# Hybrid decoder layer on one core: the gated delta rule's triangular inverse with 16x16 blocks solved on VectorE, all four token tiles together

## The reference

```python
lower = jnp.where(strict, jnp.einsum("bhnid,bhnjd->bhnij", kb, kc) * decay, 0.0)
a_mat = lower + jnp.eye(C, dtype=F32)
rhs = jnp.concatenate([vc * bc, kb * jnp.exp(gc)[..., None]], axis=-1)
sol = lax.linalg.triangular_solve(a_mat, rhs, left_side=True, lower=True, unit_diagonal=True)
```

## Time and profile before

| | us |
|---|---|
| median of 3 runs | 585.76 (583.97 to 585.95) |
| the profiled execution | 584.36 |
| its span | 582.5 |
| PE, PEld busy | 556.0, 422.6 |
| DVE, ACT, POOL busy | 263.5, 192.7, 183.2 |

### The profile page before, as it was taken

The page is one execution under the profiler, slowest core; times in us unless marked ns, Lnnn a source line. Parts: engine busy times, 40 slices in busy tenths (PEclk is TensorE's granted clock), DMA queues, the critical chain, the costliest instruction groups (busy, mean ns, idle before and its releaser), DMA issues.

```text
span 582.5 us, 11328 instructions
## 1 busy us (share of the span) xinstructions
PE 556.0 (95%) x4579; PEld 422.6 (73%) x4579; DVE 263.5 (45%) x632; ACT 192.7 (33%) x409; POOL 183.2 (31%) x126
## 2 busy tenths in 40 slices
PE   8999999999999999999999999999999999978894
PEld 6988887899999777577899996656565566544541
DVE  6598543683357334756411363322333232221126
ACT  6655545532223524446353221111111111111113
POOL 3353434164676436224534001121111112110020
PEclk9999999999999999999999999999999999999998
DMA  8865543513220320047988788999999999999975
GB/s 330 347 221 159 184 125 113 145 38 111 74 73 2 110 73 2 1 146 279 340 317 338 249 321 342 404 428 431 423 424 425 427 423 425 425 422 429 414 316 225
DMA packets 32083, 152.67 MB, mean 262 GB/s; under 512 B 8759, under 2 KB 12511, under 8 KB 25376
## 3 DMA queue, kind: packets, MB, share of 16 engines
q1 hardware_dynamic: 27360, 143.77, 63.7%
q0 software_dynamic: 4528, 8.15, 3.7%
q10 hardware_dynamic: 144, 0.03, 0.0%
HBM read 143.78 MB, written 16.27 MB: 275 GB/s over the span
## 4 chain that ended last, share of the span: by engine, by line
PE 67%; DMA 20%; DVE 4%; issue 4%; POOL 2%; ACT 2%; SPq 0%; DVEq 0%; POOLq 0%; ACTq 0%
PE bank L803 31%; DMA xg<-h2d,tok 11%; DMA w<-in_expert_w_dram 8%; PE bank L859 7%; PE bank L1249 6%; PE bank L1208 3%; PE bank L1223 2%; PE bank L828 2%; PE bank L1147 2%; PE bank L1161 1%; PE bank L1141 1%; PE bank L1261 1%; PE bank L1117 1%; POOL wlo L1578 1%; PE bank L966 1%
## 5 line engine op out<-in xcount | busy, mean ns | idle before, releaser
L1578 POOL TENSOR_TENSOR wlo<-raw,whi 128x1024 fp32r<-128x1024 f32 (+1 forms) x24 | 59.4, 2475 | 76.9 <-ACT whi L1278 72.2
L1705 POOL DMA_INDIRECT yd<-oy,dst x15 | 15.1, 1009 | 163.8 <-DVE oy L2249 153.1
L1208 PE MATMUL bank<-w,xT 128*64 128x256 f32 x512 | 58.2, 380 | 3.5 <-issue 3.5
L1223 PE MATMUL bank<-w,xT 128*64 128x256 f32 x512 | 58.2, 380 | 3.4 <-DMA w<-in_expert_w_dram 3.3
L1249 PE MATMUL bank<-w,hidT 128*64 128x512 f32 x256 | 58.5, 599 | 1.4 <-ACT hidT L1555 1.4
L1208 PEld LDWEIGHTS bank<-w,xT 128*64 128x64 f32 x512 | 37.3, 137 | 27.5 <-issue 12.0
L803 PE MATMUL bank<-wlo,hHi 128*128 128x256 f32 (+2 forms) x192 | 55.9, 291 | 0.0
L2227 DVE SCALAR_TENSOR_TENSOR hid<-bank,slot,sa 128x256 f32<-128x256 f32 x16 | 10.8, 674 | 94.5 <-issue 92.0
L1223 PEld LDWEIGHTS bank<-w,xT 128*64 128x64 f32 x512 | 36.5, 137 | 22.7 <-DMA w<-in_expert_w_dram 4.8
L803 PE MATMUL bank<-whi,hHi 128*128 128x256 f32 (+1 forms) x176 | 51.0, 290 | 0.2 <-POOL wlo L1578 0.2
L803 PE MATMUL bank<-whi,hLo 128*128 128x256 f32 (+1 forms) x176 | 49.6, 282 | 0.0
(11 more groups left out here) (388 smaller groups left out, 1132.2 us busy)
## 6 DMA issues: line engine op xcount, KB each, us to landing
w<-in_expert_w_dram SPq DMA_DIRECT2D x43, 2048.0 KB, 22.0
raw<-in_w_in_dram SPq DMA_DIRECT2D x24, 512.0 KB, 4.0
w<-in_expert_w_dram SPq DMA_DIRECT2D x10, 1024.0 KB, 7.3
yd<-zt SPq DMA_DIRECT2D x8, 512.0 KB, 5.0
yt<-yd SPq DMA_DIRECT2D x4, 1024.0 KB, 8.2
raw<-in_w_in_dram SPq DMA_DIRECT2D x6, 520.0 KB, 5.6
xt<-in_turned_dram SPq DMA_DIRECT2D x4, 512.0 KB, 6.8
X<-in_x_dram SPq DMA_DIRECT2D x4, 512.0 KB, 10.3
```

Source lines behind the costliest of these rows:

```text
L1208: m = pe.matmul(pb[3][r, 0:FF], xT[:, c, r], w1[u % 4][:, e, c * FF:(c + 1) * FF], start=(c == 0), stop=(c == KC - 1), skip_group_check=True)
L1223: m = pe.matmul(pb[7][r, 0:FF], xT[:, c, r], w3[u % 4][:, e, c * FF:(c + 1) * FF], start=(c == 0), stop=(c == KC - 1), skip_group_check=True)
L1578: pool.tensor_tensor(low_of(g), raw_of(g), high_of(g).bitcast(F32), ALU.subtract).then_inc(wlo_done, 1)
L1705: pool.indirect_dma_start(yd.ap()[:, :], bass.IndirectOffsetOnAxis(ap=dst_i[o][:, 0:1].bitcast(U32), axis=0), oy[o][:, :], None, bounds_ch ...
```

## The change

Levels 0, 1 and 2 of the inverse are no longer done by matmuls. The 16x16 diagonal blocks of all four tiles are inverted by back substitution on VectorE. `prep` masks Nm to its 16x16 blocks and sums them into `diag` (128 rows x 8 head-tiles x 16); SP writes `diag` to DRAM and reads it back in eight reads of 16 partitions each, so that each partition holds all 16 rows of its block (`spread`, one buffer for both pairs). `solve` then does 15 steps of one multiply and one sum, each waiting for the one before, and places the result in Xc. Levels 3 and 4 and the last one handle both pairs at once (8 blocks and not 4 per product, in Xc[i] with i the tile within its pair). The tasks of tiles 2 and 3 (`dec`, `decx`, `prep`) stand behind granule 18, the solves behind 19 and 21, level 3 starts behind 24, the last level behind 26, the `fin`s behind 27 and 28; nothing is left behind 29. In SP's stream the write of the blocks stands behind the load of granules 21 and 24, the reads behind 22 and 25; the second reads wait for the end of the first solve; the load of the key rows cB moves from behind 19 to behind 27. GpSimd's wait before granule 19's subtraction is for the block sums and not for the finished transposes. The core of the diff:

```diff
+SB = 16
+SOLVED = 3
...
 AFTER[17] += [("kt", 3), ("ktv", 3), ("prep", 0)]
+AFTER[17].append(("qg", 0))
+AFTER[18] += [("dec", 2), ("dec", 3), ("decx", 2), ("prep", 2)]
+AFTER[19] += [("qg", 2), ("solve", 0)]
+AFTER[21].append(("solve", 1))
 AMID = {g: {} for g in range(GR_IN)}
-for _i in range(LEVELS - 1):
-    AFTER[18 + _i].append(("lvY", 0, _i))
-    AMID[19 + _i][1] = [("lvX", 0, _i)]
-AFTER[23].append(("last", 0))
-AFTER[23] += [("dec", 2), ("dec", 3), ("decx", 2)]
-AFTER[24] += [("fin", 0), ("prep", 2)]
-for _i in range(LEVELS - 1):
-    AMID[25 + _i][2 if _i == 0 else 0] = [("lvY", 1, _i)]
-    AFTER[25 + _i].append(("lvX", 1, _i))
-AFTER[26].append(("silu",))
-AFTER[29] += [("last", 1), ("fin", 1)]
+AFTER[24].append(("lvY", 3))
+AMID[25][1] = [("lvX", 3)]
+AFTER[25].append(("lvY", 4))
+AMID[26][0] = [("lvX", 4)]
+AFTER[26] += [("lastY",), ("silu",)]
+AMID[27][0] = [("lastU",)]
+AFTER[27].append(("fin", 0))
+AFTER[28].append(("fin", 1))
+BLOCKS_OUT, BLOCKS_IN, KEYS_IN = {21: 0, 24: 1}, {22: 0, 25: 1}, 27
...
-    put("nM1", -((row % 2 == 0) & (blk == row + 1)).astype(np.float32))
+    put("blk16", -(row // SB == blk // SB).astype(np.float32))
+    put("unit16", -(row % SB == np.arange(SB)[None, :]).astype(np.float32))
     put("id64", row == blk)
     lv = []
-    for n in range(LEVELS - 1):
+    for n in range(SOLVED, LEVELS - 1):
...
+        Nm = [at(f"Nm{t}", [P, NH, P], (R4 if t < 2 else R8 + 4 * KB) + t % 2 * 2 * KB) for t in range(T)]
+        Xc, Uc, Yc = ([at(f"{n}{i}", [P, 2 * NH, HB], R4 + (o + 2 * i) * KB) for i in range(2)] for n, o in (("Xc", 4), ("Uc", 8), ("Yc", 12)))
+        Ym, Dm = ([at(f"{n}{i}", [P, NH, P], R4 + (o + 2 * i) * KB) for i in range(2)] for n, o in (("Ym", 12), ("Dm", 16)))
+        Um = [at(f"Um{i}", [P, 2 * NH, P], R4 + (16 - 8 * i) * KB) for i in range(2)]
+        spread = at("spread", [P, SB, 2 * NH, SB], R9)
...
+        eights = lambda a: sml(a, 2 * NH * SB).rearrange("p (c n) -> p c n", c=2 * NH)
+        diag, prods, inv = [eights(640), eights(768)], eights(896), eights(80)
...
+            def blocks_out(pr):
+                sp.wait_ge(rows_done, pr + 2)
+                sp.dma_start(nbd.ap()[pr], small[:, 640 + 128 * pr:768 + 128 * pr]).then_inc(s_bw, 16)
+
+            def blocks_in(pr):
+                sp.wait_ge(s_bw, 32 + 16 * (pr + 1))
+                if pr:
+                    sp.wait_ge(uinit, pr)
+                for d in range(P // SB):
+                    src = nbd.ap()[pr:pr + 1, d * SB:(d + 1) * SB, :].rearrange("o k n -> o (k n)")
+                    sp.dma_start(spread[d * SB:(d + 1) * SB, :, :, :].rearrange("p k c n -> p (k c n)"),
+                                 src.broadcast_to([SB, SB * 2 * NH * SB])).then_inc(s_spread, 16)
+
             sp.wait_ge(zero_set, 1)
             for g in range(5, GR_IN + 4):
                 granule(g)
+                if g in BLOCKS_OUT:
+                    blocks_out(BLOCKS_OUT[g])
+                if g in BLOCKS_IN:
+                    blocks_in(BLOCKS_IN[g])
                 if g == 11:
...
-                if g == 19:
+                if g == KEYS_IN:
+                    sp.wait_ge(uinit, 2)
                     keys_in()
...
-                for h in range(NH):
+                for c in range(2 * NH):
                     for i in range(2):
                         for r in (UP, DN):
-                            m = mm(banks[i][out(i, r), h * HB:(h + 1) * HB], stationary(i, h, r), moving(i, h, r))
-                            if h == NH - 1 and r is DN:
+                            m = mm(banks[i][out(i, r), c * HB:(c + 1) * HB], stationary(i, c, r), moving(i, c, r))
+                            if c == 2 * NH - 1 and r is DN:
                                 end(m, names[i])
...
+                    lv = k[1]
+                    if lv > SOLVED:
+                        for i in range(2):
+                            wait_read(pe, ("Xp", i, lv - 1))
+                    else:
+                        pe.wait_ge(uinit, 2)
+                    quarters([("Y", i, lv) for i in range(2)], lambda i, c, r: Nm[2 * (c // NH) + i][r, c % NH, r],
+                             lambda i, c, r: Xc[i][r, c, :], lambda i, r: OTHER[r.start] if i else r)
...
+                    pe.wait_ge(u_turned, lv - SOLVED + 1)
+                    quarters([("Xp", i, lv) for i in range(2)], lambda i, c, r: Uc[i][r, c, :],
+                             lambda i, c, r: Yc[i][r, c, :], lambda i, r: OTHER[r.start] if i else r)
...
+                elif k[0] == "lastU":
+                    lv = LEVELS - 1
                     for i in range(2):
-                        t = 2 * pr + i
-                        wait_read(pe, ("Y", t, lv))
-                        pe.wait_ge(um_low, t + 1)
-                        blocks(("Up", t, lv), lambda h, r, o: mm(o, Yc[i][DN, h, :], Um[i][DN, h, DN]), (UP,))
+                        name = ("Up", i, lv)
+                        wait_read(pe, ("Y", i, lv))
+                        pe.wait_ge(um_low, i + 1)
+                        ps = begin(name)
+                        for c in range(2 * NH):
+                            m = mm(ps[UP, c * HB:(c + 1) * HB], Yc[i][DN, c, :], Um[i][DN, c, DN])
+                        end(m, name)
                 elif k[0] == "fin":
...
-                    if k[1] == 0:
-                        decay_rows(0)
+                    decay_rows(k[1])
...
-                if k[0] == "prep":
+                if k[0] == "qg":
...
-                elif k == ("decx", 0):
-                    masked(0)
-                    masked(1)
+                elif k[0] == "decx":
+                    for t in (k[1], k[1] + 1):
+                        if k[1]:
+                            wait_read(pool, ("KK", t - 2))
+                        masked(t)
...
-                if ("fin", 0) in AFTER[g]:
-                    for t in (2, 3):
-                        wait_read(pool, ("Up", t - 2, LEVELS - 1))
-                        masked(t)
-                for t in (0, 2):
-                    if ("prep", t) in AFTER[g]:
-                        pool.wait_ge(uinit, t + 2)
+                if ("prep", 0) in AFTER[g]:
+                    pool.wait_ge(rows_done, 2)
...
+                    if t >= 2:
+                        wait_read(dve, ("QK", t - 2))
...
+                    pr = k[1] // 2
+                    blocks = Uc[pr]
                     for i, t in enumerate(tiles):
                         wait_read(dve, ("KK", t))
                         for r in (UP, DN):
-                            j = dve.tensor_tensor(Yc[i][OTHER[r.start] if i else r, :, :], Nm[i][r, :, r], half(const("nM1"), r), ALU.mult)
+                            j = dve.tensor_tensor(blocks[r, NH * i:NH * i + NH, :], Nm[t][r, :, r],
+                                                  const("blk16")[r, :].unsqueeze(1).broadcast_to([HB, NH, HB]), ALU.mult)
                     link(j)
-                    for i in range(2):
-                        j = dve.tensor_tensor(Uc[i], Yc[i], id64.unsqueeze(1).broadcast_to([P, NH, HB]), ALU.add)
-                    link(j)
-                    dve.transpose(Xc[0], Uc[0]).then_inc(uinit, 1)
-                    dve.transpose(Xc[1][UP, :, :], Uc[1][DN, :, :])
-                    dve.transpose(Xc[1][DN, :, :], Uc[1][UP, :, :]).then_inc(uinit, 1)
+                    dve.tensor_reduce(diag[pr], blocks[:, :, :].rearrange("p c (d n) -> p c n d", n=SB), AX_X, ALU.add).then_inc(rows_done, 1)
...
+                elif k[0] == "solve":
+                    pr = k[1]
+                    unit = const("unit16").unsqueeze(1).broadcast_to([P, 2 * NH, SB])
+                    if pr:
+                        dve.wait_ge(uinit, pr)
+                    dve.tensor_copy(inv[:, :, SB - 1:SB], unit[:, :, SB - 1:SB])
+                    link(dve.tensor_copy(prods, unit))
+                    dve.wait_ge(s_spread, 16 * (P // SB) * (pr + 1))
+                    for b in reversed(range(SB - 1)):
+                        link(dve.tensor_tensor(prods[:, :, b + 1:], inv[:, :, b + 1:], spread[:, b, :, b + 1:], ALU.mult))
+                        link(dve.tensor_reduce(inv[:, :, b], prods[:, :, b:], AX_X, ALU.add))
+                    places = const("blk16", "p (d n) -> p d n", dict(n=SB)).unsqueeze(1).broadcast_to([P, NH, HB // SB, SB])
+                    for i in range(2):
+                        rows = inv[:, NH * i:NH * i + NH, :].unsqueeze(2).broadcast_to([P, NH, HB // SB, SB])
+                        j = dve.tensor_tensor(Xc[i][:, NH * pr:NH * pr + NH, :].rearrange("p h (d n) -> p h d n", n=SB), rows, places, ALU.mult)
+                    j.then_inc(uinit, 1)
+                    if pr:
+                        dve.wait_ge(uinit, 2)
+                        turn()
...
+            def turn():
+                dve.transpose(Uc[0][:, :, :], Xc[0][:, :, :])
+                dve.transpose(Uc[1][DN, :, :], Xc[1][UP, :, :])
```

(54 more changed lines are left out.)

104 lines of the change are left out of this document (46 added, 58 removed).

## The result

The changed kernel takes 590.42 us (median of 4 runs, 589.55 to 592.68) where the kernel before takes 585.63 on the same chip: a ratio of 1.0094, 95% interval 1.0060 to 1.0128. It is slower by 0.9%. The profiled execution took 589.55 with a span of 587.7, 5.2 longer than before.

What follows compares the result with a forecast made beforehand. TensorE, busy 95% of the span, was taken to bound the kernel; -11.1 + 1.9 + 13.8 + 1.7 + 1.0 = +7.3 on 584.4 gave 591.7, forecast as 592 us. Its own range was 586 to 597; 8 of 10, 576 to 598.

Steps and rivals of the forecast that it cites:

- rival (a): Solves on VectorE are not held up by GpSimd, solve 1 ends near 168; -8.2 us, 576; chance 0.24.
- (b): Solves held up by half, TensorE's wait 6 to 9 us; +0.3 us, 585; chance 0.14.
- (c): Late granule 26 weights or a broadcast read over 10 us stretch TensorE's wait to 20; 598; chance 0.10.
- What leaves TensorE: Input projection: levels 0 to 2 go, fewer restarts in levels 3 and 4, waits at the last level go; -11.1 us.
- The last level and the final products keep their matmuls: End of the block inverse on TensorE: matmuls unchanged, so only the waits there were counted as saved, 0.9 us.
- First new wait: Before granule 24, TensorE waits for its weights, as GpSimd's rotation delays their subtraction; 1.9 us.
- Second new wait: Before the first level piece, TensorE waits for the two VectorE solves held up by GpSimd; 13.8 us, bounds 11 to 15.
- the bound of 9: Upper bound in us for the second blocks' read after solve 0; bounds 3 and 9, 6 taken.
- the signs: What would show the forecast, including solve multiplies of 1 us and more wherever GpSimd is busy, sums never.
- Granule 26's weights: Raw weights behind SP's wait: issued at 164, landed by 173, needed by TensorE after 190, so hidden.
- The clock: After TensorE's idle of 13.8 us the granted clock drops; 1.7 us, between 0 and 3.1.
- Behind the projection: At attention's start, later norm scaling and last subtraction on GpSimd hold VectorE's normalizing; 1 us, between 0 and 2.5.

Runs made afterwards that it cites:

- e1: Changed kernel with the solve's unknowns (inv) in a PSUM bank instead of SBUF; 578.5 us, ratio 0.9903 to the kernel before.
- e3: Changed kernel with a second buffer for the rows of the second read, inv still in SBUF; 588.58 us, ratio 1.0075 to the kernel before.
- e2: Changed kernel with 115 extra matmuls keeping TensorE busy before its wait for the solves; 589.12 us, ratio 1.0100 to the kernel before.
- e11: The changed kernel run once more, unaltered; 590.70 us, ratio 1.0108 to the kernel before.
- e10: Changed kernel with GpSimd's norm scaling moved behind granule 27, nothing else; 588.79 us, ratio 1.0067 to the kernel before.
- e4: Changed kernel with levels 3, 4 and the last level each a granule or more later; 580.09 us, ratio 0.9930 to the kernel before.
- e5: Changed kernel with GpSimd's rotations moved from behind granules 21 and 23 to behind 25 and 27; 588.63 us, ratio 1.0076 to the kernel before.
- e8: Changed kernel with inv in PSUM and rotations behind granules 25 and 27, one buffer; time 0.2 above its expected range of 577.5 to 579.5 us.
- e7: Changed kernel with inv in PSUM and a second read buffer, rotations unmoved; time within its expected range of 576 to 578.5 us.
- e6: Changed kernel with inv in PSUM, second read buffer and rotations behind granules 25 and 27; time within its expected range of 572.5 to 575 us.
- e9: e6 plus norm scaling behind granule 27 and the second rotation behind 26 instead of 27; 572.18 us, ratio 0.9792 to the kernel before.

## Why the prediction was right

Forecast +7.3 on the profiled execution and 592 us; measured +5.2 and 590.4. The mechanism was the forecast's, shown by e1; rival (a) is excluded by the held multiplies, (b) and (c) by the wait's size. By the steps:

- **What leaves TensorE: -11.1 forecast, -14.4 measured**, as 3.0 less 13.24, 2.50 and the clock's 1.65. This term was mis-sized most. Counted from start to start in the two timelines, the granules' own matmuls give 2.4 (16 restarts, forecast at 2.6), the waits that went 1.1, as forecast, and the level pieces 8.2 and not 7.4: twenty pieces of 0.62 to 0.70 became four of 1.09, where the forecast left twice 0.62 for each. "The last level and the final products keep their matmuls" was the largest miss: the last level was put at nothing beside its waits, and gave 2.2 (6.2 before, 4.0 after, waits left out). It has the same 128 records, but the change also issues them in another order. TensorE's timeline of the kernel before, then of the changed one:
```profile
166.45 0.97 PE L859 MATMUL bank<-Xm,Nm 64*64 64x64 f32 x13
...
167.37 0.98 PE L859 MATMUL bank<-CT,Xm 64*64 64x64 f32 x27
```
```profile
201.29 0.27 PE L880 MATMUL bank<-Xc,Nm 64*64 64x64 f32 x1
201.30 0.27 PE L880 MATMUL bank<-CT,Xc 64*64 64x64 f32 x2
```
Before, each pair had 16 records of the product, all in one quarter of the array, and then 32 of the transposes, in two: 1.9 us per pair. In the changed kernel the loop takes one matmul of each in turn, in three quarters, and all 96 records take 2.09 from 201.29. The second product, in one quarter in both kernels, took 1.05 for 16 records and takes 2.00 for 32: the longer run by itself saves next to nothing. The remaining 0.4 or so lies in the other products and ahead of 129 us.
- **First new wait: 1.9 forecast, 2.5 measured.** The rotation took 7.2 us, not 6.9 (154.24 to 161.46), and the subtraction behind it 2.53, not 2.4. VectorE's held instructions are the cause: in e1, where they are not held, the two take 6.9 and 2.35 and the wait is 1.9.
- **Second new wait: 13.8 forecast, 13.24 measured, partly by errors that cancel.** Solve 0 ended at 161.8, not 163.5, as the placing multiplies met the rotation's end and not a full subtraction. The read took 9.9 us from issue to use, not 6, which is beyond the bound of 9 and at the edge of rival (c). Since it took longer, solve 1 missed most of the second rotation and was held in two places, not three or four: 11.4 us from 171.79 to 183.2 against 13 forecast. So solve 1 ended within 0.2 us of the forecast, which was luck, and TensorE came 0.8 later (170.0 and not 169.2). e3 shows the trade. Of the signs, one was off in size: beside the rotation the multiplies took 0.77 to 0.78, not "1 us and more".
- **Granule 26's weights: hidden, as forecast.** Their issue waited until 165.76 and ScalarE had them at 172.98.
- **The clock: 1.7 forecast, 1.65 measured** (1.99 - 1.16 for the level piece, and 3.82 instead of 3.0 for the half granule behind it); e2 has the same 1.16 at the upper level. That this would be the midpoint of the bounds was luck; the second profile (e11) lost 2.4 there.
- **Behind the projection: 1.0 forecast, 1.0 measured** to the mix transposes, its cause confirmed by e10; another execution of the same kernel (e11) has 2.0, inside the forecast's 0 to 2.5.
- **The whole: terms of -14.4, 2.5, 13.24, 1.65 and 1.0 give +4.0**, the first xT matmul is 4.05 later, and 1.1 more fell behind it. That is no effect of the change: from the first xT matmul to the end the span has 233.2 us before, 234.4 in the first profile of the changed kernel and 233.0 in its second, and 232.7 to 234.8 over all kernels here. So the forecast was 2.1 too high by the removal's 3.3, less this 1.1; what is left, 0.6 more at the rotation and 0.6 less at the solves, cancels.

## What to carry to other kernels

When a chain of short VectorE operations is put beside GpSimd, find what GpSimd does then and count SBUF operands: each multiply or sum of two tensors that reads both from SBUF may cost the rest of a GpSimd instruction, and an operand in PSUM frees it at the same 0.2 to 0.3 us each. Copies and tensor_scalar operations from SBUF to SBUF were held here too (2.2 and 1.1 us). Work taken off the busiest engine is worth only what the chain that now feeds it allows: write down when the last link ends, and place its reader behind that. After a fix, look for what is late next before counting on a second: here the rotations' move was worth nothing until the read was early. And compare two profiles of one kernel before an effect of 1 or 2 us is put down to an edit: a wait of 2 to 3 us brought the lower clock in some executions and not in others.

## What the runs showed of the hardware that was not expected

- A broadcast read of 1 MB in 8 DMAs, each repeating 8 KB rows into 16 partitions, took 9.9 to 10.3 us from the first issue to the first use in seven kernels (the changed one, e1, e2, e4, e5, e8, e10), 3.9 of them for issuing, and 10.7, 11.1 and 11.3 in e7, e6 and e9. The DMA engines were fully busy at 130 GB/s (165 to 170 us), where the expert weights move at over 420 (measured over slices of the page). Why was not tested.
- The clock is not a function of the program alone: behind the wait for wlo it stayed at 1.00 in the changed kernel's first profile and was 0.68 over 165 to 170 us in its second. Behind waits of 1.9 to 2.5 us at this place six profiles (e1 to e4, e10, e11) show 0.67 to 0.71, and two (the first, and e7) 1.00. So a wait of 2 us may cost more than itself: TensorE reached level 3 1.3 us later in e11. The same holds behind the 2.6 us wait for vb (it fell in six profiles of eight) and behind e4's 2.6 us wait for the solve.
- A copy of 8 elements per partition, SBUF to SBUF, was held like the multiplies, though it has one input (2.21 and 2.23 us beside a subtraction); into PSUM, beside a subtraction too, it took 0.17.
- Matmuls of 64x64 in one quarter of the array start 0.058 us apart per record, and quarters run side by side when the issue order takes them in turn: 0.06 us per record with one quarter, 0.03 with two, 0.02 with three (the last level, above).
